# Products into the residual: the high half of the weights meets both halves of the operand in one 512-column matmul

## What is computed

```
# first network, layer 0 (even mixer): y_a from a convolution branch, y_b from a recurrence
x = x + gate0 * (concat([y_a, y_b]) @ ev_w_out)          # 2048 -> 1024: "ya" and "yb"
# layer 1 (odd mixer): y from pooling windows, a grouped product and a gate
x = x + gate1 * ((y * silu(g)) @ od_w_out)               # 2048 -> 1024: "oa" and "ob"
x = rmsnorm(x, final_g)
# second network: gated linear recurrence and spatial gating, merged
x = x + gate2 * (merged @ w_o)                           # 1024 -> 1024: "wo"
x = x + gate3 * ((silu(a) * b) @ w_down)                 # 2816 -> 1024: "d0", "d1", "d2"
x = rmsnorm(x, g_final)
```

## Time and profile before

| | us |
|---|---|
| median of 3 runs (904.73, 906.09, 908.63) | 906.09 |
| span of the profiled execution, first to last instruction | 903.1 |
| time of that execution beside its span | not given apart; the median lies 3.0 above the span |
| TensorE busy | 884.7 (98%) |
| TensorE weight loads | 829.2 (92%) |
| VectorE busy | 710.0 (79%) |
| ScalarE busy | 504.7 (56%) |
| GpSimd busy | 142.2 (16%) |

### The profile page before, as it was taken

How to read it: one execution, slowest core, us unless ns; L and a number is a source line. 1 busy time by engine, 2 the same in 40 slices (tenths; PEclk the granted TensorE clock), 3 DMA queues, 4 the chain that set the end, 5 groups by cost and what they waited for, 6 DMA issues and landing times.

```text
span 903.1 us, 17404 instructions
## 1 busy us (share of the span) xinstructions
PE 884.7 (98%) x7132; PEld 829.2 (92%) x7132; DVE 710.0 (79%) x1033; ACT 504.7 (56%) x727; POOL 142.2 (16%) x254
## 2 busy tenths in 40 slices
PE   8999999999999999999999999999999999999996
PEld 6688776689999999989999999999999999999995
DVE  5689667989888999968569975797987998765543
ACT  5474888997845455225554465483535644444441
POOL 0003864710021001300211100300001000000000
PEclk9999999999999999999999999999999999999998
DMA  9946987885776677866638844555556567666661
GB/s 365 388 144 216 306 271 222 280 274 181 214 276 210 230 262 269 293 215 201 184 103 292 303 128 142 178 173 187 155 180 181 172 204 255 187 185 183 196 204 52
DMA packets 55295, 195.45 MB, mean 216 GB/s; under 512 B 7856, under 2 KB 7984, under 8 KB 53808
## 3 DMA queue, kind: packets, MB, share of 16 engines
q1 hardware_dynamic: 39600, 147.73, 50.4%
q0 software_dynamic: 15616, 46.61, 15.2%
HBM read 188.60 MB, written 1.05 MB: 210 GB/s over the span
## 4 chain that ended last, share of the span: by engine, by line
PE 75%; DVE 14%; ACT 4%; issue 3%; DMA 2%; POOL 1%; DVEq 0%; SPq 0%; ACTq 0%; POOLq 0%
PE ps L582 22%; PE ps L584 21%; PE ps L583 21%; DVE w_lo L1415 4%; PE ps L756 3%; PE ps L685 2%; PE px L674 2%; ACT w_hi L980 1%; DVE win L1429 1%; DVE dump L1788 1%; DMA x<-in_xT 1%; DMA raw<-in_stream 1%; DVE li L1429 1%; PE px L861 1%; DVE li L1614 1%
## 5 line engine op out<-in xcount | busy, mean ns | idle before, releaser
L1415 DVE TENSOR_TENSOR w_lo<-raw,w_hi 128x1024 fp32r<-128x1024 f32 x232 | 280.5, 1226 | 83.9 <-ACT w_hi L980 83.3
L980 ACT ACTIVATE w_hi<-raw 128x1024 fp32r<-128x1024 f32 x232 | 242.7, 1055 | 110.8 <-DMA raw<-in_stream 110.0
L582 PE MATMUL ps<-h_hi,w_hi 128*128 128x256 f32 (+1 forms) x864 | 256.0, 296 | 6.2 <-DVE w_lo L1415 2.8
L583 PE MATMUL ps<-h_lo,w_hi 128*128 128x256 f32 (+1 forms) x864 | 251.4, 291 | 0.0
L584 PE MATMUL ps<-h_hi,w_lo 128*128 128x256 f32 (+1 forms) x864 | 251.3, 291 | 0.0
L582 PEld LDWEIGHTS ps<-h_hi,w_hi 128*128 128x128 f32 x864 | 165.3, 191 | 16.6 <-issue 5.7
L583 PEld LDWEIGHTS ps<-h_lo,w_hi 128*128 128x128 f32 x864 | 165.4, 191 | 3.5 <-issue 1.2
L584 PEld LDWEIGHTS ps<-h_hi,w_lo 128*128 128x128 f32 x864 | 165.4, 191 | 2.7
L459 POOL DMA_DIRECT2D modw<-in_mod_w x80 | 42.8, 536 | 391.6 <-DVE modw L1449 250.1
L582 PE MATMUL ps<-h2o_hi,w_hi 128*128 128x256 f32 x352 | 101.5, 288 | 0.0
L584 PE MATMUL ps<-h2o_hi,w_lo 128*128 128x256 f32 x352 | 99.6, 283 | 0.0
(11 more groups left out here) (353 smaller groups left out, 1856.6 us busy)
## 6 DMA issues: line engine op xcount, KB each, us to landing
raw<-in_stream SPq DMA_DIRECT2D x252, 512.0 KB, 3.8
modw<-in_mod_w POOLq DMA_DIRECT2D x80, 512.0 KB, 5.7
m<-in_mod_w SPq DMA_DIRECT2D x8, 1024.0 KB, 19.5
shifts<-upad POOLq DMA_DIRECT2D x128, 35.5 KB, 4.7
c_row<-in_c_rows SPq DMA_DIRECT2D x3, 512.0 KB, 7.6
ctxT<-in_ctxT SPq DMA_DIRECT2D x1, 1024.0 KB, 4.9
x<-in_xT SPq DMA_DIRECT2D x1, 1024.0 KB, 7.1
ctx2T<-in_ctx2T SPq DMA_DIRECT2D x1, 1024.0 KB, 6.5
```

The lines of the kernel that those rows point to most:

```text
L582: pe.matmul(o, wh, hi, start=start, stop=False)
L583: pe.matmul(o, wh, lo, start=False, stop=False)
L980: act.activation(w_hi[split[0] % HI_RING][:], raw[n % RING][:], ACT.Copy).then_inc(w_hi_ready, 1)
L1415: v.tensor_tensor(w_lo[n % RING][:], raw[n % RING][:], w_hi[split[0] % HI_RING][:].bitcast(F32), ALU.subtract).then_inc(w_lo_ready, 1)
```

## The change

Both halves of an operand get one tensor of two equal parts (`pair`), so that `at_tile` can name both halves of a k tile as one 512-column operand. `h_hi` and `h_lo` become parts of one `h`. Most halves keep their places; `m_hi` moves from 60 to 52 KiB (above W), `m_lo` from 88 to 60, `y_lo` from 97.25 to 94. `thirds` becomes `halved`, with the same three matmuls, for the products that don't go into the residual; `thirds` itself is kept for the product of x that isn't normed.

For tiles 0 to 6 of ya, yb, oa, ob, wo, d0, d1 and d2, `in_residual` gives `twofold`: the weights' high half meets both operand halves in one matmul of 512 columns, which fills the whole bank: columns 0 to 255 get high x high, columns 256 to 511 high x low. The weights' low half still adds its 256 columns to the first. VectorE then adds both halves of the bank to x in two steps, with a wait between them. Tile 7 stays as it was.

```diff
+        def pair(name, kib, apart, tiles):
+
+            both = at(name, kib, [2, int(256 * apart)], F32R)
+            return both, *(both[:, e, 0:tiles * T].rearrange("p (k t) -> p k t", t=T) for e in range(2))
+
+        def at_tile(both, k):
+
+            return both[:, :, k * T:(k + 1) * T]
+
...
+            def products(o, wh, wl, both, start, stop):
+
+                return three(o, wh, wl, both[:, 0, :], both[:, 1, :], start, stop)
+
+            def halved(name, t, both, ready=None, tiles=KT, first=True, last=True):
...
+            def twofold(name, t, both, ready=None, tiles=KT, first=True, last=True):
+
+                wh, wl = split_weights(name, t)
+                o = bank_of(name, t) if first else psum_of(name, t)
+                for k in range(tiles):
+                    if ready is not None:
+                        pe.wait_ge(ready[0], ready[1] + k + 1)
+                    operand, at_end = both(k), last and k == tiles - 1
+                    if at_end:
+                        pe.matmul(o[:, 0:T], wl[:, k, :], operand[:, 0, :], start=False, stop=False)
+                    mm = pe.matmul(o[:, :], wh[:, k, :], operand, start=first and k == 0, stop=at_end)
+                    if not at_end:
+                        mm = pe.matmul(o[:, 0:T], wl[:, k, :], operand[:, 0, :], start=False, stop=False)
+                mm.then_inc(tile_done, 1)
+
+            def in_residual(t):
+
+                return twofold if t < KT - 1 else halved
...
             for t in range(4):
-                thirds("ya", t, *ya, last=False, ready=(ya_ready, 0) if t == 0 else None)
+                twofold("ya", t, ya, last=False, ready=(ya_ready, 0) if t == 0 else None)
             for t in range(4):
-                thirds("yb", t, *yb, first=False, ready=(yb_ready, 0) if t == 0 else None)
+                twofold("yb", t, yb, first=False, ready=(yb_ready, 0) if t == 0 else None)
             for t in range(4, KT):
-                thirds("ya", t, *ya, last=False)
+                in_residual(t)("ya", t, ya, last=False)
             for t in range(4, KT):
-                thirds("yb", t, *yb, first=False)
+                in_residual(t)("yb", t, yb, first=False)
...
@@ in add_to_x
                 v.wait_ge(tile_done, TILE[(name, t)] + 1)
                 xt = x[:, t, :]
+                if t < KT - 1:
+                    S.do(v.scalar_tensor_tensor(out=xt, in0=psum_of(name, t)[:, T:2 * T], scalar=gate[:, t:t + 1],
+                                                in1=xt, op0=ALU.mult, op1=ALU.add))
+                    S.sync()
                 v.scalar_tensor_tensor(out=xt, in0=psum_of(name, t)[:, 0:T], scalar=gate[:, t:t + 1],
                                        in1=xt, op0=ALU.mult, op1=ALU.add).then_inc(free_of(name, t), 1)
```

More of the change, by code:

```diff
@@ L209, in build @@
         ga = at("ga", W, [KT, T])
-        ya_hi = at("ya_hi", W, [KT, T], F32R)
+        ya_both, ya_hi, ya_lo = pair("ya_both", W, 48, KT)
         conv = at("conv", W + 8, [KT, T])
@@ L219, in build @@
         gb = at("gb", W + 16, [KT, T])
[L220 to L222 removed]
+        yb_both, yb_hi, yb_lo = pair("yb_both", W + 24, 16, KT)
         LB = 4
@@ L592, in thirds, with side_by_side @@
                         pe.wait_ge(ready[0], ready[1] + k + 1)
-                    mm = three(o[:, 0:width], wh[:, k, :], wl[:, k, :], hi(k), lo(k), first and k == 0,
-                               last and k == tiles - 1)
+                    mm = products(o[:, 0:T], wh[:, k, :], wl[:, k, :], both(k), first and k == 0, last and k == tiles - 1)
                 mm.then_inc(tile_done, 1)
-            def side_by_side(tiles, hi, lo, ready, take=True, last=True):
+            def twofold(name, t, both, ready=None, tiles=KT, first=True, last=True):
[13 more added lines that the diff above has]
+                return twofold if t < KT - 1 else halved
+            def thirds(name, t, hi, lo, width, ready):
+                wh, wl = split_weights(name, t)
+                o = bank_of(name, t)
+                for k in range(KT):
+                    if ready is not None:
+                        pe.wait_ge(ready[0], ready[1] + k + 1)
+                    mm = three(o[:, 0:width], wh[:, k, :], wl[:, k, :], hi(k), lo(k), k == 0, k == KT - 1)
+                mm.then_inc(tile_done, 1)
+            def side_by_side(tiles, both, ready, take=True, last=True):
                 for k in range(KT):
@@ L603, in side_by_side @@
                         o = bank_of(name, t) if k == 0 and take else psum_of(name, t)
-                        mm = three(o[:, 0:T], wh[:, k, :], wl[:, k, :], hi(k), lo(k), k == 0, last and k == KT - 1)
+                        mm = products(o[:, 0:T], wh[:, k, :], wl[:, k, :], both(k), k == 0, last and k == KT - 1)
                         if k == KT - 1:
@@ L662, in _, with own @@
                     xb(t, k)
-            own = (lambda k: h_hi[:, 1, k, :], lambda k: h_lo[:, 1, k, :])
+            def own(k):
+                return h[:, :, 1, k, :]
             def gates(head):
@@ L689, in va_vg @@
             def va_vg(t):
-                thirds("va", t, *own)
-                thirds("vg", t, *own)
+                halved("va", t, own)
+                halved("vg", t, own)
             va_vg(0)
@@ L742, in _, with h1 @@
             keep_busy(14)
-            h1 = (lambda k: h1_hi[:, k, :], lambda k: h1_lo[:, k, :])
-            side_by_side([("ou", t) for t in range(4)], *h1, (h_ready, 0))
+            def h1(k):
+                return at_tile(h1_both, k)
+            side_by_side([("ou", t) for t in range(4)], h1, (h_ready, 0))
             for t in range(4, 2 * KT):
-                thirds("ou", t, *h1)
+                halved("ou", t, h1)
             for t in range(2 * KT):
-                thirds("og", t, *h1)
+                halved("og", t, h1)
             two_chunks(px[1], sqx, 2, 2 * KT)
@@ L778, in _, with own2 @@
                     two_chunks(px[2], sqc, 4, 4 * KT)
-            side_by_side([("f", t) for t in range(4)], lambda k: h2o_hi[:, k, :], lambda k: h2o_lo[:, k, :],
-                         (h_ready, 2 * KT), take=False)
+            def own2(k):
+                return at_tile(h2o_both, k)
+            side_by_side([("f", t) for t in range(4)], own2, (h_ready, 2 * KT), take=False)
             def both_tokens(name, t):
@@ L785, in both_tokens @@
                 o = bank_of(name, t)
-                for s in range(2):
-                    hi, lo = both[s]
+                for s, both in enumerate((h2o_both, h2c_both)):
                     for k in range(KT):
-                        mm = three(o[:, s * T:(s + 1) * T], wh[:, k, :], wl[:, k, :], hi[:, k, :], lo[:, k, :], k == 0,
-                                   k == KT - 1)
+                        mm = products(o[:, s * T:(s + 1) * T], wh[:, k, :], wl[:, k, :], at_tile(both, k), k == 0, k == KT - 1)
                 mm.then_inc(tile_done, 1)
@@ L927, in _ @@
             for t in range(2, KT):
-                thirds("gb2", t, *own2)
+                halved("gb2", t, own2)
             for t in range(HEADS):
-                for name, hi, lo, ready in (("pa", oa_hi, oa_lo, oa_ready), ("pb", ob_hi, ob_lo, ob_ready)):
+                for name, both, ready in (("pa", oa_both, oa_ready), ("pb", ob_both, ob_ready)):
                     wh, wl = split_weights(name, t)
```

131 lines of the change are left out of this document (62 added, 69 removed).

## The result

The changed kernel is slower: 912.0 us, median of 20 runs (908.87 to 920.19), beside 906.08 for the kernel before (20 runs, 904.73 to 913.86). The ratio is 1.007, with a 95% interval from 1.0051 to 1.009. The forecast was 908.0, and its range ended at 911.5.

A forecast was written before the change was run, and what follows sets the result against it. TensorE, 98% busy, was taken as the bound, with VectorE-ScalarE rings setting the ends of yb and ob. ya/yb +1.5, oa/ob +2.6, wo -0.15, down -2.05 gave +1.9 us: 908.0, range 903 to 911.5.

The forecast's parts named there:

- The ring: In ya/yb and oa/ob VectorE and ScalarE wait for each other in turn, 3.11 and 3.51 us a turn.
- the second step's price: VectorE's added step into x costs 0.52 us per tile (bounds 0.48 and 0.57), on 28 tiles of yb, ob, wo, down.
- turns of 3.6 and 4.0: Expected sign of being right: VectorE's step-to-step time in yb and ob grows to 3.6 and 4.0 us.
- the steps hidden in down: In down the second steps hide beside the next tile's matmuls, so the stage comes out at -2.05 us.
- the absorbed wait: ScalarE's DMA wait before the fifth w_hi swallows turns 0 to 3's delay in yb and gives back 1.0 in ob.
- The half microsecond allowed for the absorbed waits: Part of the forecast's own range, 906.5 to 909.5, beside -0.6 and +0.7 for the step's price.
- the size of the merge: One 512-column matmul for two of 256 saves TensorE 13.3 ns, 434 times: 5.8 us, 2.05 of it in down.
- The bound from below: Lower limit on a merged pair's saving on TensorE: nothing saved, as the same columns stream; 13.3 ns was taken.
- a rival of 0.02: The merge saves nothing behind a narrow matmul: down gives 0, the sum is 910.1; chance 0.02.
- the 3.0 us around the span: Time outside the profiled span for the median run: 903.1 to 906.09 before, 905.0 to 908.0 forecast.
- rival (c): Slower: the granted clock falls in new pauses before the norms of yb and ob, adding 3 us: 911; chance 0.14.
- Rival (a): VectorE's added steps are hidden and TensorE's 5.8 us saving counts whole: 900.3, faster; chance 0.11.

The follow-up runs named there:

- experiment 2: Changed kernel without VectorE's second step into x (high x low product left out for tiles 0 to 6): 904.71 us, ratio 0.999 to the kernel before.
- experiment 3: Changed kernel with each wide matmul split into two of 256 columns, both VectorE steps kept: 912.36 us, ratio 1.0072 to the kernel before.
- Experiment 4: Changed kernel with each tile's wide matmuls in one row and its narrow ones in another: 915.89 us, ratio 1.0104 to the kernel before.
- experiment 12: The changed kernel itself run again, for more runs and another profile: 912.43 us, ratio 1.0075 to the kernel before.
- experiment 1: Changed kernel with the change kept in down alone; ya, yb, oa, ob, wo back to narrow matmuls and one step: 907.54 us, ratio 1.0003.
- 5: Changed kernel with ScalarE's high halves five tiles ahead instead of four in yb and ob: 904.81 us, ratio 0.9986.
- 7: Changed kernel with ScalarE five tiles ahead in yb and ob, and wide and narrow matmuls in blocks except wo 0: 904.62 us, ratio 0.9991.
- 8: Changed kernel with 10 more filler matmuls in TensorE's pauses at each of the norms of yb and ob: 916.15 us, ratio 1.0105.
- 9: Changed kernel with ScalarE five tiles ahead in yb and ob for t < 7, four for the last tile: 906.07 us, ratio 0.9983.
- 10: Changed kernel with ScalarE's lead five tiles, four for the last, and matmuls in blocks except wo 0: 904.2 us, ratio 0.9984.
- 6: Kernel before, with ScalarE's high halves five tiles ahead instead of four in yb and ob: 906.22 us, ratio 0.9992.
- 11: Kernel before, with ScalarE five tiles ahead in yb and ob, four for the last tile: 905.64 us, ratio 0.9995.

## Why the prediction was wrong

**The mechanism was right.** The ring, the second step's price (0.51 measured, 0.52 taken), turns of 3.6 and 4.0, new waits of 1.45 at the norm of yb and 1.06 and 1.72 at that of ob, on banks at ya 6 and 7 and oa 7 (0.16, 0.66 and 0.81), the steps hidden in down: all are in the profile. (The 1.45 and the 1.06 are put down to GpSimd's sum of the squares and not to ScalarE's last square; L551 follows right behind the last square at both norms.) Experiments 2 and 3 show it from both sides: the loss goes with the steps and stays without the wide matmuls. wo came at -0.26, for -0.15.

**First failed step, the absorbed wait.** The prediction let the fifth `w_hi`'s wait for its DMA swallow turns 0 to 3 whole ("step 4 stands at 273.75 as before"). ScalarE's wait was indeed swallowed, but VectorE had no such wait to give: its block of five `w_lo` began 1.13 us later than before (268.79 for 267.66) and had 0.36 of slack from its start to the step behind it (6.14 us before, 5.78 after). Step 4 was 0.77 late, where the prediction had it in its old place. In ob the block began 2.09 later within its stage and had 0.28 of slack (5.97 before, 5.69 after), where the prediction let 1.0 be given back. The stages came out at +2.40 for +1.5 and at +3.37 for +2.6. The block of five explains 0.7 to 0.8 of each of the two differences, and some 0.2 in ya/yb lie between the norm's last matmul and the next product (5.27 for 5.05). The half microsecond allowed for the absorbed waits was too little.

**Second failed step, the size of the merge.** 13.3 ns came from runs of equal matmuls. In alternation a pair saves 7.7 ns: down came at -1.18 for -2.05, another +0.87. The bound from below ("nothing saved") was in the text, but drawn into the range only as a rival of 0.02. Experiment 4 shows that turning between widths takes 3.7 of the missing 5.6 ns.

Together these make +4.33 instead of +1.9, a median of 910.4 if the executions were spread alike, which is inside the range of 903 to 911.5. **Third failed step, the 3.0 us around the span**, taken over from the kernel before for the median run. The executions are not spread alike: the changed kernel's median lies 4.6 above its profiled span. The medians are 5.9 apart, the two lowest runs 4.1 and the two profiled executions 4.4. In the changed kernel 8 of 20 runs lie at 915 or above, in the kernel before none. One part is rival (c): the granted clock did fall behind the norm of ob in two of the four profiles with waits of 0.9 to 1.1 and of 1.7 us there (in experiments 3 and 12, not in the first profile and 4). In the changed kernel that cost 2.76 us, beside the 3 that the rival gave for both norms; its 6 to 7 us at the lower level came from no row, and some 6.8 us stood there in experiment 12 (474.0 to 480.8), behind one norm. In none of the profiles without these two waits did the clock fall there. The waits of TensorE there (1.06 and 1.72) add up to more than that at yb (1.45), where fillers run and no profile shows a fall. The Trainium skill (TensorE: Matmul & The Clock Gate, "HAM oscillation") has waits for DMAs between bursts of matmuls, longer ones than these, bring the array back to half rate. Two profiles show the same behind these shorter pauses, and the first one, with the same pauses, does not.

In the one high run that was profiled, the larger part (8.45 of 11.4 us) is the late modulation DMA ahead of 102 us. It meets other kernels too: experiments 1, 2 and 4 start ya at 238.3 to 238.6, and three runs of the kernel before reached 911 to 914 in the last experiment. The wider spread is still there when the ring is open. In the ten sets of runs with wide matmuls (the changed kernel, 1, 2, 4, 5, 7 to 10 and 12) 58 of 115 runs lie more than 3 us above the fastest of their set, in those without (the four sets of the kernel before, 3, 6 and 11) 30 of 146. So it goes with the wide matmuls rather than with the second steps or the pauses at the norms, even where they stand in down alone (6 of 12 in experiment 1). This is a count over all sets and not a test: experiment 3, which has the steps without the wide matmuls, has 11 runs. Why wide matmuls should go with a delay at 100 us stays open: nothing ahead of 235 us was changed in what is computed, and no run tells.

Rival (a), VectorE's steps hidden, was wrong for this kernel. With the ring open (experiments 9 and 11) the steps are hidden in oa/ob too, and TensorE's saving counts there, but in all at some 2.4 to 2.85 us instead of 5.8.

## What to carry to other kernels

Where a DMA wait absorbs a delay, ask which queue ends next once it is gone: sum up every block of work between the delayed step and the next one, on each engine, and take the latest. A price read from rows of equal instructions need not hold for a mix of unequal ones. Before work is handed to an engine that looks idle for a fifth of the time, see whether it is a link of a ring: there 0.5 us is paid in each turn, until the neighbour is given one more tile of lead.

## What the runs showed that was not expected

A 512-column matmul and a 256-column one in alternation start 353 ns apart as a pair, where rows of their own kind give 226.7 + 120.0 = 346.7; in blocks within the same stage 348.6 (360 less the 11.4 saved). At the 1.2 GHz level the 256-column matmuls behind the norm of ob started 213 ns apart (478.19, 478.40 in the last profile), for 120 at 2.4. And the same pause in the same kernel, 1.7 us ahead of L551 with two matmuls before it, let the clock fall in one execution and not in another. The same holds near 105 us: a wait of 1.84 us for a `w_lo` was followed by a clock of 0.50 in experiment 2, and one of 3.10 in experiment 1 was not.
